# Low halves of the gated FFN rows on GpSimd, and work of the next stage placed around the last down product, in a two-layer encoder trunk

## The reference

```python
h = _rmsnorm(x, g_pre_mix[l]) * (1 + sc1) + sh1
m = _mixer(h, ...)                       # z = h @ w_in, attention, spatial gating, w_out
x = x + ga1 * _rmsnorm(m, g_post_mix[l])
h = _rmsnorm(x, g_pre_ffn[l]) * (1 + sc2) + sh2
f = (jax.nn.silu(h @ w_gate[l]) * (h @ w_up[l])) @ w_down[l]
x = x + ga2 * _rmsnorm(f, g_post_ffn[l])
```

## Time and profile before

| | |
|---|---|
| median of three runs | 3814.08 us |
| span of the profiled execution | 3804.7 us |
| TensorE busy | 3386.0 us, 89% |
| VectorE, GpSimd, ScalarE busy | 1797.6, 1426.3, 1038.8 us |
| mean granted TensorE clock | 0.953 |
| first FFN | from 968 to 1987 us of the span |
| second FFN | from 2788 us to the end |

### The profile page before, as it was taken

The page is one execution under the profiler, slowest core; times in us unless marked ns, Lnnn a source line. Parts: engine busy times, 40 slices in busy tenths (PEclk is TensorE's granted clock), DMA queues, the critical chain, the costliest instruction groups (busy, mean ns, idle before and its releaser), DMA issues. The chain is left out here.

```text
span 3804.7 us, 48831 instructions
## 1 busy us (share of the span) xinstructions
PE 3386.0 (89%) x19532; PEld 3033.0 (80%) x19532; DVE 1797.6 (47%) x2807; ACT 1038.8 (27%) x2298; POOL 1426.3 (37%) x804
## 2 busy tenths in 40 slices
PE   5998888888999998999988978888899999899997
PEld 2987677767888888888878777776788888888886
DVE  3116777754444534534433156786443453453333
ACT  2323555553100001200014234776320110120001
POOL 2210687810654544444530302000054454455441
PEclk7998899989999999999999988998999999999998
DMA  6205444422322223322222134112232222242222
GB/s 202 71 15 160 143 146 147 150 78 88 101 74 77 72 73 89 99 69 72 73 60 100 55 123 119 29 34 67 76 117 72 67 74 77 72 131 75 72 67 67
DMA packets 397728, 337.90 MB, mean 89 GB/s; under 512 B 107192, under 2 KB 325000, under 8 KB 397504
## 3 DMA queue, kind: packets, MB, share of 16 engines
q1 hardware_dynamic: 249808, 233.18, 20.1%
q10 hardware_dynamic: 147696, 101.61, 9.2%
HBM read 282.87 MB, written 51.87 MB: 88 GB/s over the span
## 5 line engine op out<-in xcount | busy, mean ns | idle before, releaser
L581 POOL TENSOR_SCALAR w_hi<-raw 128x1024 fp32r<-128x1024 f32 (+2 forms) x400 | 458.7, 1147 | 2270.2 <-PE ps L598 2135.0
L583 POOL TENSOR_TENSOR w_lo<-raw,w_hi 128x1024 fp32r<-128x1024 f32 (+2 forms) x400 | 975.4, 2438 | 33.4
L596 PE MATMUL ps<-w_lo,ht_hi 128*128 128x512 f32 (+2 forms) x2040 | 798.5, 391 | 145.8 <-DVE tokm L1685 83.3
L596 PE MATMUL ps<-ht_lo,w_hi 128*128 128x320 f32 x2816 | 873.3, 310 | 4.9 <-DVE ht_lo L1359 3.0
L597 PE MATMUL ps<-ht_hi,w_lo 128*128 128x320 f32 x2816 | 871.6, 310 | 0.0
L598 PE MATMUL ps<-ht_hi,w_hi 128*128 128x320 f32 x2816 | 871.5, 309 | 0.0
L597 PE MATMUL ps<-w_hi,ht_lo 128*128 128x512 f32 (+2 forms) x2040 | 787.1, 386 | 0.0
L598 PE MATMUL ps<-w_hi,ht_hi 128*128 128x512 f32 (+2 forms) x2040 | 784.9, 385 | 0.0
L596 PEld LDWEIGHTS ps<-w_lo,ht_hi 128*128 128x128 f32 x2040 | 397.8, 195 | 232.5 <-DVE tokm L1685 99.0
L596 PEld LDWEIGHTS ps<-ht_lo,w_hi 128*128 128x128 f32 x2816 | 530.0, 188 | 8.1 <-DVE ht_lo L1359 3.8
L597 PEld LDWEIGHTS ps<-ht_hi,w_lo 128*128 128x128 f32 x2816 | 530.0, 188 | 1.6
(11 more groups left out here) (127 smaller groups left out, 3681.2 us busy)
## 6 DMA issues: line engine op xcount, KB each, us to landing
raw<-in_w_gate_dram SPq DMA_DIRECT2D x88, 512.0 KB, 3.8
raw<-in_w_up_dram SPq DMA_DIRECT2D x88, 512.0 KB, 3.8
raw<-in_w_down_dram SPq DMA_DIRECT2D x88, 512.0 KB, 3.5
raw<-in_w_mod_dram SPq DMA_DIRECT2D x80, 512.0 KB, 4.3
x_rows<-tokm ACTq DMA_DIRECT2D x30, 512.0 KB, 5.0
x_old<-x_rows ACTq DMA_DIRECT2D x30, 512.0 KB, 4.3
kv_rows<-stage ACTq DMA_DIRECT2D x20, 512.0 KB, 3.3
tokm<-kv_rows ACTq DMA_DIRECT2D x30, 320.0 KB, 4.1
```

Source lines behind the costliest of these rows:

```text
L581: pool.tensor_scalar(hi, r, 1.0, 0.0, ALU.mult, ALU.add).then_inc(s_whi, 1)
L583: pool.tensor_tensor(lo, r, hi.bitcast(F32), ALU.subtract).then_inc(s_w, 1)
L596: pe.matmul(out, lhs[0], rhs[1], start=first, stop=False)
```

## The change

- **Low halves on GpSimd.** `gated_low` leaves VectorE. GpSimd gets `gated_lows(upto)`, which it calls ahead of the gate piece and the up piece of tile b, for all tiles up to b-2, and ahead of the next layer's first pieces.
- **Norms behind the adds.** `norm_waiting` moves from ahead of the products to behind the adds.
- **Second half.** k = 2 and 3 are turned ahead too, in tiles 20 and 21. The last down product of the first half is issued inside the second half: gate of tile 0 on six k, transposes of k = 0, the last down product, transposes of k = 1, up on six k, then both on k = 0 and 1.
- **Next layer.** Likewise the last down product of a layer stands inside the next: z of four token tiles on k = 2 and 3, transposes of k = 0 and 1, the last down product, z on k = 4 to 7, z on k = 0 and 1.
- **Loads.** The next layer's columns and gains are loaded one per tile instead of all at the start of the second half, and ScalarE's wait for the adds moves into `residual`.

```diff
@@ GpSimd
+            def gated_lows(upto):
+                while lows[0] < upto:
+                    b = lows[0]
+                    half, j = divmod(b % (2 * FT), FT)
+                    for c in range(2):
+                        pool.wait_ge(s_ah, 2 * b + c + 1)
+                        hi, lo = (x[:, c * 320:(c + 1) * 320] for x in act_ring(half, j % 4))
+                        pool.tensor_tensor(lo, gated32[:, c, :], hi.bitcast(F32), ALU.subtract).then_inc(s_al, 1)
+                    lows[0] += 1
+
             for i, (src, m, n, (hi, lo), (kind, l, b)) in enumerate(pieces):
+                if kind == "gate_up" and b >= 2:
+                    gated_lows(tile_no(l, 0, b - 1))
+                if kind == "block" and b == 0 and l:
+                    gated_lows(tile_no(l, 0, 0) - (last_piece[(l, 0, 3)] > i))
@@ order of the transposes
-        EARLY_K = range(4, KT)
+        LATE_K = (0, 1)
-        DEFERRED = {("tb", 0, 3): 5, ("z", 0, 0): 6, ("z", 0, 1): 7, ("tb", 1, 7): 8, ("z", 0, 4): 9}
+        DEFERRED = {("tb", 0, 1): 5, ("z", 0, 0): 6, ("z", 0, 1): 7, ("tb", 1, 7): 8, ("z", 0, 4): 9}
+        AHEAD = {5: [(0, 4)], ..., 15: [(1, 6), (1, 7)],
+                 20: [(0, 2), (1, 2)], 21: [(0, 3), (1, 3)]}
+        NEXT_AHEAD = {9: 4, 11: 5, 13: 6, 15: 7, 20: 2, 21: 3}
+        FIRST_KS = (4, 5, 6, 7, 2, 3)
+        Z_PARTS = ((2, 3), (4, 5, 6, 7))
@@ TensorE, start of the next layer
+                if l:
+                    pe.wait_ge(s_ht, tb_no[("mix", l, 0, 3)] + 1)
+                    pe.wait_ge(s_sil, 2 * tile_no(l, 0, 0))
+                    pe.wait_ge(s_a32, 2 * tile_no(l, 0, 0))
+                    for t in range(4):
+                        bank(("z", l, 0, t))
+                    z_first(l, Z_PARTS[0], False)
+                    for k in LATE_K:
+                        transposes(("mix", l, 0, k), [row_block(i, k) for i in range(4)])
+                    down(l - 1, 1, PAIRS - 1)
+                    z_first(l, Z_PARTS[1], False)
+                    pe.wait_ge(s_ht, ht_count("mix", l, 0))
+                    z_first(l, LATE_K, True)
@@ TensorE, FFN
                     for m in range(PAIRS):
-                        gate_up(2 * m)
+                        if half and m == 0:
+                            pe.wait_ge(s_ht, tb_no[("ffn", l, 1, 1, 3)] + 1)
+                            gate_up(1, 0, FIRST_KS, (0,), True, False)
+                            for gi in range(2):
+                                transpose_ffn(("ffn", l, 1, gi, LATE_K[0]))
+                            down(l, 0, PAIRS - 1)
+                            for gi in range(2):
+                                transpose_ffn(("ffn", l, 1, gi, LATE_K[1]))
+                            gate_up(1, 0, FIRST_KS, (1,), True, False)
+                            pe.wait_ge(s_ht, ht_count("ffn", l, 1))
+                            gate_up(1, 0, LATE_K, (0, 1), False, True)
+                        else:
+                            gate_up(half, 2 * m, range(KT), (0, 1), True, True)
                         if m:
-                            down(m - 1)
+                            down(l, half, m - 1)
...
-                    down(PAIRS - 1)
+            down(L - 1, 1, PAIRS - 1)
@@ ScalarE
             def residual(l, which, t):
                 waiting.append((l, which, t))
...
+                if which:
+                    act.wait_ge(s_acc, DPP * (pair_no(l, t // HT_, PAIRS) - 1) + 2 * (t % HT_ + 1))
                 tile_std(t, ST_TILE + 2 * (res_no(l, which, t) % 2))
...
-                            load_cols(l + 1, 0)
-                            load_gains(l + 1)
+                        if l + 1 < L and half == 0 and j < 5:
+                            load_gains(l + 1, j)
+                        if l + 1 < L and half == 1 and j < 5:
...
+                            load_cols(l + 1, 0, j)
...
-                    act.wait_ge(s_acc, DPP * pair_no(l, half, PAIRS))
@@ VectorE
+                else:
+                    add_down(l - 1, 1, PAIRS - 1)
                 for n, e in enumerate(z_order(l)):
...
                     if half:
-                        for gi in range(2):
-                            for k in range(KT):
-                                if k not in EARLY_K:
-                                    split_row_bank(("ffn", l, 1, gi, k))
+                        add_down(l, 0, PAIRS - 1)
+                        for k in LATE_K:
+                            for gi in range(2):
+                                split_row_bank(("ffn", l, 1, gi, k))
...
                         for j in (2 * m, 2 * m + 1):
-                            norm_waiting()
                             for c in range(2):
                                 gated_product(j, c)
-                            for c in range(2):
-                                gated_low(j, c)
                             if j % 2 == 0 and m:
-                                add_down(m - 1)
+                                add_down(l, half, m - 1)
+                            norm_waiting()
```

More of the change, by code:

```diff
@@ L236, in interleaved @@
             return out
-        EARLY_K = range(4, KT)
+        LATE_K = (0, 1)
         def z_order(l):
-            out = [("tb", 0, k) for k in range(KT) if l == 0 or k not in EARLY_K]
+            out = [("tb", 0, k) for k in range(KT) if l == 0 or k in LATE_K]
             out += [("z", 0, t) for t in range(4)]
@@ L833, in _, with gate_up @@
                             ins.then_inc(rdy[b], 1)
-                for half in range(2):
[L836 to L841, removed]
+                def gate_up(half, j, ks, parts, first, last):
+                    jj = tile_no(l, half, j)
+                    tok0 = half * HTOK
+                    for i in parts:
+                        name, done, read = (("w_gate", s_g, s_sil), ("w_up", s_u, s_a32))[i]
+                        if first:
+                            pe.wait_ge(s_w, last_piece[(l, name, half * FT + j)])
+                        for c in range(2):
+                            if jj and first:
+                                pe.wait_ge(read, 2 * (jj - 1) + c + 1)
+                            for k in ks:
+                                rhs = [h[:, k, tok0 + c * 320:tok0 + (c + 1) * 320] for h in (ht_hi, ht_lo)]
+                                ins = product(ps[:, 2 * i + c, 0:320], [x[:, k, :] for x in w_gu(j, i)], rhs, first and k == ks[0], last and k == ks[-1])
+                            if last:
+                                ins.then_inc(done, 1)
+                for half in range(2):
+                    if half == 0:
                         for t in (NT - 2, NT - 1):
@@ L861, in down @@
[L861 to L872, removed]
@@ L876, in _ @@
                         if m:
[L877 to L878 removed]
+                            down(l, half, m - 1)
+                        for key in ahead(l, half, 2 * m):
+                            transpose_ffn(key)
+                        gate_up(half, 2 * m + 1, range(KT), (0, 1), True, True)
                         for key in ahead(l, half, 2 * m + 1):
                             transpose_ffn(key)
[L881 removed]
+            down(L - 1, 1, PAIRS - 1)
@@ L1402, in next_rows, with add_down @@
                 dve.tensor_scalar(x_tile(t), x_tile(t), c, None, ALU.mult).then_inc(s_xn, 1)
+            def add_down(l, half, m):
+                for n in range(DPP):
+                    t, c = divmod(n, 2)
+                    k = DPP * pair_no(l, half, m) + n
+                    dve.wait_ge(s_dn, k + 1)
+                    f = tokm[:, c, half * HT_ + t, :]
+                    if m:
+                        dve.wait_ge(s_acc, k - DPP + 1)
+                        dve.tensor_tensor(f, ps[:, 4 + n % 2, :], f, ALU.add).then_inc(s_acc, 1)
+                    else:
+                        dve.tensor_copy(f, ps[:, 4 + n % 2, :]).then_inc(s_acc, 1)
+                    if m == PAIRS - 1 and half == 1 and l == L - 1 and c and t:
+                        residual(l, 1, HT_ + t - 1)
             for t in range(2, 4):
```

120 lines of the change are left out of this document (59 added, 61 removed).

## The result

The changed kernel takes 3682.85 us (median of four runs, 3675.31 to 3686.46). The kernel before, with one more run of it in the same comparison, takes 3812.92 us (3810.03 to 3815.51). The ratio is 0.966, with a 95% interval of 0.964 to 0.968: 130 us, or 3.4%, less. The forecast was 3692 us, within 3670 to 3728.

What follows compares the result with a forecast made beforehand. TensorE, busy 89% of the span, was taken as the bound, stalled by adds queued behind low halves. Gains 97.8 + 17 + 9 - 2 - 0.3 = 121.5 us off the 3804.7 span, plus 9.4, gave 3692 us, range 3670 to 3728.

Steps and rivals of the forecast that it cites:

- Low halves and adds: Down products: TensorE's 39 waits on VectorE's adds vanish once the low halves go to GpSimd, gaining 97.8 us.
- the clock: Granted TensorE clock, lowered behind stalls, stays up: 17 us gained, bounds 10 and 20.
- Norms: Odd tiles: norms moved behind the adds cost 0, or up to 12 us if the long stalls come back.
- the three long stalls: Three of the 39 waits on adds, 6 us each, where a norm waiting for a row's store precedes the products.
- Half boundary: Between a layer's halves, twice: 44 us falls to 39.4, gaining 4.6 each, 9 in all; bounds -2 and +9 each.
- Layer boundary: Between the layers, once: 66 us against 63.8, taken as 0 less 2 for the clock; bounds -7 and +4.
- signs of being wrong: Waits on the adds that stay, GpSimd late with weights, or a layer boundary shorter by more than 4 us.
- sign of being right: Layer 1: TensorE stands 12 to 15 us ahead of the transposes of the second group.
- The 2 us for the clock: Layer boundary: 2 us lost to the lower clock behind TensorE's long idle time.
- The end: Last low half of all, on an idle GpSimd, 0.3 us later than before: -0.3 us.
- The offset: Median of the runs, 3814.1 us, lies 9.4 above the profiled span, 3804.7; carried over to the forecast.
- boundaries come out well: Rival at the boundaries: splits free of GpSimd, shorter chain, clock stays up; 3674 us, chance 0.12.

Runs made afterwards that it cites:

- both holds: Changed kernel with GpSimd's weight conversions made to wait for VectorE's splits at the half boundary and at the layer boundary: 3664.81 us.
- the hold: Changed kernel with GpSimd's first conversion of the second half waiting until row 3 of the new tokens is split: 3671.57 us, 0.963.

## Why the prediction was right, and where its sum was off

**Low halves and adds: right.** The 39 waits are gone, and the halves without their boundaries gave 118.1 us. The forecast was 97.8 for the stalls and 17 for the clock. The difference, 118.1 - 97.8 = 20.3, lies just above the upper bound given for the clock (20), as one would expect when the granted clock stays at 1.00 throughout. The cause is what stands ahead of the adds in VectorE's queue: moving the low halves behind them within VectorE gives 112 us, taking them off VectorE gives 126. The prediction gave the gain to both steps in one and did not say that the order alone would do. GpSimd's low half, estimated at 0.85 us, in the changed kernel (durations min, median and max in ns):

```profile
L563 POOL TENSOR_TENSOR ht_lo<-gated,ht_hi x176: 856/879/1815, 998.1 to 3638.8; 128x320 fp32r<-128x320 f32 x176
```

0.88 us against 0.48 on an undisturbed VectorE is 1.8 times. It did not matter, as VectorE had needed 1.1 us in the median. The Trainium skill (GPSIMD Engine Reference, section Engine selection) gives a factor of about 2 for two inputs, and these rows come near it.

**Norms: right at 0.** None of the three long stalls came back. The runs add that this part has no gain of its own here.

**Half boundary: right in kind, 0.9 us each too little.** Gate began 7.4 us behind up (8.2 forecast), VectorE's held splits were what set it, and the boundaries fell by 5.4 and 5.6 us (4.6). Of the 0.9, 0.8 are these splits; from the first gate on, 31.2 us were forecast, and 31.2 and 30.9 came. The order of before already gives 2.1 of the 5.5 once the low halves are on GpSimd (41.8 us). This is a term that the forecast had only inside its total of 44: the last down product of a half has to wait for its own low halves. In the trace of before, TensorE at the half boundary and at the layer boundary:

```profile
1446.90 0.58 PE L596 MATMUL ps<-w_lo,ht_hi 128*128 128x512 f32 x1 [4.15 <-DVE ht_lo L1675]
...
1970.05 0.80 PE L596 MATMUL ps<-w_lo,ht_hi 128*128 128x512 f32 x1 [3.40 <-DVE ht_lo L1675]
```

With the low halves on GpSimd and the old order, the same wait at the layer boundary:

```profile
1895.25 0.50 PE L614 MATMUL ps<-w_lo,ht_hi 128*128 128x512 f32 x1 [2.02 <-POOL ht_lo L560]
```

**Layer boundary: the step that failed.** Forecast 0 less 2, measured a gain of 5.0. That is above the bound of 4, and a layer boundary shorter by more than 4 us was one of the prediction's own signs of being wrong. The sum was 26 us until down is over, 8.3 until the chain of residuals, and 31.5 less some 3 for the chain. The trace has 24.2, 7.6 and 27.0, which is 58.8. So every term of the sum was too long, by 1.8, 0.7 and 1.5 us. The sum itself gave 62.8, which is 1 us less than before, and the forecast took 0 and then 2 off for the clock. TensorE's long idle time of "some 14 us" is 9.2 there, under the 12 to 15 named as a sign of being right. The 2 us for the clock do not show. It did fall behind the idle time (0.81 over 1946 to 1975 us), but there the chain, and not TensorE, sets the end:

```profile
1933.68 1.50 DVE L1445 SCALAR_TENSOR_TENSOR tokm<-tokm,stat,gate_row 128x1024 f32<-128x1024 f32 x1
...
1959.89 0.75 DVE L1468 TENSOR_SCALAR tokm<-tokm,stat 128x1024 f32<-128x1024 f32 x1 [0.89 <-DMA x_rows<-tokm]
```

That the reordering itself is worth nothing there was right, but not by the forecast's count. With the low halves on GpSimd and the old order the boundary is 58.8 us too. There down starts 1.4 us earlier than in the kernel before, and it runs at full clock (1.00 over 1895.2 to 1902.0). In the kernel before, the granted clock was 0.50 over the first 6.8 us of it (1969.4 to 1976.2), behind the wait of 3.40 us. The window around that product:

```profile
1966.00:1987.00 21.00, 17.60 (x68) 14.11 (x67) 9.65 (x13) 0.47 (x1) 5.61 (x4) 0.84 0.13 35
```

That is 0.16 x 21 = 3.4 us of clock. So the chain starts 27.9 us behind up instead of 32.2. The new order starts it at 31.8 and wins as much inside the chain. What the forecast did not have at all is the wait on ScalarE (L1090), 6.5 us, quoted with TensorE's waits above. ScalarE's timeline there, a sum of squares for a residual ahead of the release of a z bank:

```profile
1948.54 1.06 ACT L956 ACTIVATE squares<-tokm 128x1024 bf16<-128x1024 f32 x1 [6.17 <-DVE tokm L1447]
...
1951.78 0.47 ACT L1090 ACTIVATE ps<-ps 128x384 f32<-128x384 f32 x1
```

It costs nothing here, as the norm comes later still.

**The end: -3.0 instead of -0.3.** The first add of the last down product comes 5.1 us behind up (3.6 before) and the second 1.9 behind it instead of 1.4. GpSimd's low half is 0.4 us longer (0.3 forecast), so TensorE waits for it for 2.02 us instead of 1.61. What the sum lacked is the clock behind that wait: it is 0.54 over 3639.7 to 3643.4 us, where the kernel before has 1.00 over 3762.3 to 3766.0. Kernels with the low halves on VectorE end in 44.2 to 44.7 us. Of those with them on GpSimd, issued once, four show this fall of the clock and take 46.6 to 47.2; the one without it (both holds) takes 45.1.

**The offset: a wrong step that cost little.** 9.4 us were carried from the span to the median as if they lay around the span. Around the changed kernel's span lie 1.8. In every execution on record that lists both, of the kernel before too, they are 1.7 to 1.8. So its profiled execution was 7.6 us faster than the median, which the page alone could not tell. Against the median itself the forecast gain was 121.5 us, and 130.1 came. The 8.6 between are the terms above: 3.3 in the halves, 1.8 and 7.0 at the boundaries, less 2.7 at the end, 9.4 in all (the stretches give 1.0 more than the medians). That misses of opposite sign partly cancel is luck.

Of the rivals, "boundaries come out well" was nearest, and the measured time lies as close to its 3674 us as to the forecast's 3692. The layer boundary came 5 us better than before, while the half boundaries still collided. What that rival wanted of the splits, an idle GpSimd, was worth 8.3 us for the two, as the hold showed.

## What to carry to other kernels

When a producer waits for a consumer on a busy queue, look at what stands ahead of the release in that queue, before moving work to another engine. Here two lines moved within one engine gave 112 of 130 us. The second engine then pays where the two run at the same time on a path that sets the end. There, holding back the engine that has room (by 1.56 us, for weights wanted a tile later) was worth 4 us each time. And an engine's spare time can be measured by issuing its cheap instruction several times.

## What the runs showed of the hardware that was not expected

A 128x256 cast on VectorE, 0.28 us alone, took 2.42 us beside one GpSimd subtraction of 2.52 us. In the rows of the kernel with the low halves on VectorE behind the adds, the two subtractions beside GpSimd's subtractions (2.34 us) are 2.0 and 2.1 us longer than in the rows of the hold, and the casts beside GpSimd's casts (1.28 and 1.35 us) 0.6 and 0.85. So in these rows a meeting cost at most about one instruction of the other engine, whatever the size of one's own. With four low halves in a row on GpSimd (0.88 us each, ahead of the conversions of 1.05 and 2.4 us), the half boundaries were even 1.1 to 1.3 us shorter than with one (37.2 against 38.6 and 38.3): there the two splits met the short instructions and were all but done when the conversions began (1426.18). The same four rows of VectorE in that kernel:

```profile
1422.70 0.73 DVE L1430 CAST ht_hi<-tbank 128x384 fp32r<-128x384 f32 x1 [1.10 <-ACT tbank L1006]
1423.46 1.10 DVE L1431 TENSOR_TENSOR ht_lo<-tbank,ht_hi 128x384 fp32r<-128x384 f32 x1
1424.48 0.94 DVE L1430 CAST ht_hi<-tbank 128x256 fp32r<-128x256 f32 x1
1425.46 1.03 DVE L1431 TENSOR_TENSOR ht_lo<-tbank,ht_hi 128x256 fp32r<-128x256 f32 x1
```
